# Attention scores contracted over 66 and 96 partitions in place of a zero-padded 128

## The reference

```python
# first stack, layer 0: forgetting attention, 8 heads of 64
s = einsum("bqhd,bkhd->bhqk", q, k) * 64**-0.5
s = s + cum[:, :, lo:hi, None] - cum[:, :, None, :hi]   # decay, a term of the query and one of the key
p = softmax(where(causal, s, -1e30));  o = p @ v
...
# second stack, layers 0 and 1: 8 query heads of 96, 2 key groups, three branches
s_cmp = q_c . kc ;  o_cmp = softmax(s_cmp) @ vc          # 31 compressed keys
s_slc = q_c . k_slc ; s_win = q_c . k_win                # causal; with 512 tokens both cover all keys
o = g0 * o_cmp + g1 * o_slc + g2 * o_win
```

## Time and profile before

| | |
|---|---|
| time, median of 3 runs | 3630.98 us (3629.97 to 3632.04) |
| the profiled execution's own time | 3629.97 us |
| its span in the profile | 3628.2 us |
| TensorE busy | 3544.8 us, 98% of the span |
| VectorE, ScalarE, GpSimd busy | 1464.8, 1194.2 and 54.3 us |
| mean granted TensorE clock | 0.979 of full speed |

### The profile page before, as it was taken

One profiled execution on the slowest core, in us unless ns is written; L12 is line 12 of the kernel. 1 busy time (PEld: TensorE's weight loads), 2 busy tenths in 40 slices (PEclk: granted clock), 3 DMA queues, 4 the chain that ended last, 5 costly groups with the idle time before them and its releaser, 6 DMA issues.

```text
span 3628.2 us, 39774 instructions
## 1 busy us (share of the span) xinstructions
PE 3544.8 (98%) x17601; PEld 2981.9 (82%) x17601; DVE 1464.8 (40%) x1604; ACT 1194.2 (33%) x1755; POOL 54.3 (1%) x66
## 2 busy tenths in 40 slices
PE   8999999999999999999999899999999999899999
PEld 7778788888888888888888778888888888788887
DVE  4444433337644323322344454223422354553233
ACT  3344332236534222322233343222322332432222
POOL 2000000000000000000000000000000000000000
PEclk9999999999999999999998799999999998899999
DMA  5214132223341322232223102322332222013321
GB/s 158 93 47 146 52 116 93 105 76 99 105 140 61 108 93 97 87 119 93 94 80 104 47 12 93 105 93 93 105 102 96 93 78 83 24 36 121 99 93 58
DMA packets 246333, 326.44 MB, mean 90 GB/s; under 512 B 18320, under 2 KB 215232, under 8 KB 246160
## 3 DMA queue, kind: packets, MB, share of 16 engines
q1 hardware_dynamic: 241232, 308.77, 26.3%
q0 software_dynamic: 4928, 15.12, 1.2%
HBM read 321.74 MB, written 2.10 MB: 89 GB/s over the span
## 4 chain that ended last, share of the span: by engine, by line
PE 91%; DVE 5%; ACT 4%; DMA 0%; issue 0%; POOL 0%; DVEq 0%; ACTq 0%; POOLq 0%
PE P L483 27%; PE P L484 27%; PE P L485 27%; PE P L488 3%; PE P L631 3%; PE P L609 3%; DVE WR L1429 1%; ACT WR L954 1%; DVE BIG L1437 1%; ACT BIG L961 1%; DVE BIG L1446 1%; DVE HT L1437 1%; ACT XN L961 0%; PE P L868 0%; ACT BC L961 0%
## 5 line engine op out<-in xcount | busy, mean ns | idle before, releaser
L1429 DVE TENSOR_TENSOR WR<-STG,WR 128x2048 fp32r<-128x2048 f32 (+2 forms) x300 | 669.5, 2232 | 1382.1 <-ACT WR L954 1381.8
L483 PE MATMUL P<-HT,WR 128*128 128x512 f32 (+1 forms) x3016 | 1126.4, 373 | 5.5 <-DVE WR L1429 3.0
L484 PE MATMUL P<-HT,WR 128*128 128x512 f32 (+1 forms) x3016 | 1122.9, 372 | 0.0
L485 PE MATMUL P<-HT,WR 128*128 128x512 f32 (+1 forms) x3016 | 1122.6, 372 | 0.0
L954 ACT CAST WR<-STG 128x2048 fp32r<-128x2048 f32 (+2 forms) x300 | 557.5, 1859 | 1102.1 <-PE P L485 1101.9
L483 PEld LDWEIGHTS P<-HT,WR 128*128 128x128 f32 x3016 | 571.3, 189 | 105.2 <-DVE WR L1429 3.8
L485 PEld LDWEIGHTS P<-HT,WR 128*128 128x128 f32 x3016 | 570.9, 189 | 98.4
L484 PEld LDWEIGHTS P<-HT,WR 128*128 128x128 f32 x3016 | 571.2, 189 | 97.4
L483 PE MATMUL P<-WR,HT 128*128 128x512 f32 (+1 forms) x1344 | 524.6, 390 | 12.3 <-DVE HT L1437 12.3
L485 PE MATMUL P<-WR,HT 128*128 128x512 f32 (+1 forms) x1344 | 521.6, 388 | 0.0
L484 PE MATMUL P<-WR,HT 128*128 128x512 f32 (+1 forms) x1344 | 521.3, 388 | 0.0
(11 more groups left out here) (177 smaller groups left out, 2522.8 us busy)
## 6 DMA issues: line engine op xcount, KB each, us to landing
STG<-in_w_ffn_gu_dram SPq DMA_DIRECT2D x44, 1024.0 KB, 5.0
STG<-in_ffn_w_gate_dram SPq DMA_DIRECT2D x44, 1024.0 KB, 5.3
STG<-in_ffn_w_up_dram SPq DMA_DIRECT2D x44, 1024.0 KB, 5.3
STG<-in_ffn_w_down_dram SPq DMA_DIRECT2D x44, 1024.0 KB, 4.9
STG<-in_w_ffn_down_dram SPq DMA_DIRECT2D x22, 1024.0 KB, 4.8
STG<-in_w_xkv_dram SPq DMA_DIRECT2D x16, 1024.0 KB, 5.4
STG<-in_w_in_dram SPq DMA_DIRECT2D x12, 1024.0 KB, 5.2
STG<-in_w_xq_dram SPq DMA_DIRECT2D x8, 1024.0 KB, 5.2
```

The source lines that it names most:

```text
L483: pe.matmul(o, lh, rh, start=first, stop=False)
L484: pe.matmul(o, lh, rl, start=False, stop=False)
L485: return pe.matmul(o, ll, rh, start=False, stop=last)
L1429: v.tensor_tensor(WR[0:p, n % NWR, 1, cut], STG[0:p, n % NSTG, cut], WR[0:p, n % NWR, 0, cut].bitcast(F32), ALU.subtract).then_inc(ve.sem, ...
```

## The change

The score products of fox read rows 0 to 65 of queries and keys alone, and those of n0 and n1 rows 0 to 95 alone. The memsets of the zeros go, and so do the two waits of GpSimd that kept the ones behind the zeros in fox, GpSimd's wait ahead of the zeros in n0 and n1, and TensorE's wait for these zeros. The products' columns, their number and their order stay.

```diff
-        N_QP = BIG[:, 0:4096].rearrange("p (h n) -> p h n", h=8)
-        N_KP = BIG[:, 4096:6144].rearrange("p (z g n) -> p z g n", z=2, g=2)
...
-                         qk=[(F_QA[:, h, tcol(t)], F_KA[:, h, 0:128 * (t + 1)])],
+                         qk=[(F_QA[0:66, h, tcol(t)], F_KA[0:66, h, 0:128 * (t + 1)])],
...
-                         qk=[(N_QP[:, h, tcol(t)], N_KP[:, br, h // 4, 0:128 * (t + 1)])],
+                         qk=[(N_Q[:, h, tcol(t)], N_K[:, br, h // 4, 0:128 * (t + 1)])],
...
             g.wait_ge(*ve.at("positions"))
-            po.memset(F_QA[64:128, :, :], 0.0).then_inc(pw_zero.sem, pw_zero.up("zeros_q"))
-            g.wait_ge(*pw_zero.at("zeros_q"))
             po.memset(F_QA[64:66, :, :], 1.0).then_inc(pw_zero.sem, pw_zero.up("ones_q"))
             g.wait_ge(*ve.at("fox", "yb", 3))
-            po.memset(F_KA[64:128, :, :], 0.0).then_inc(pw_zero.sem, pw_zero.up("zeros_k"))
-            g.wait_ge(*pw_zero.at("zeros_k"))
             po.memset(F_KA[64:66, :, :], 1.0).then_inc(pw_zero.sem, pw_zero.up("ones_k"))
...
-                    if part == 1:
-                        g.wait_ge(*ve.at(before, "slot", 21))
-                        po.memset(BIG[96:128, 0:6144], 0.0).then_inc(pw_zero.sem, pw_zero.up("zeros", s))
...
                 scores(0)
-                g.wait_ge(*pw_zero.at("zeros", s))
                 last_turn = attend(s, lambda it: ve.at(s, "k", 2), ve.at(s, "v", 3), hook)
```

## The result

| | median of the runs | lowest to highest |
|---|---|---|
| before | 3631.21 us (9) | 3626.55 to 3632.07 |
| after | 3665.44 us (9) | 3640.06 to 3667.96 |

The ratio is 1.0078, 95% interval 1.0055 to 1.0100: slower by 0.8%. The nine executions of the changed program are not spread evenly: six lie between 3664 and 3668 us, three between 3640 and 3650. The profiled one took 3667.70 us, 37.7 more than the profiled one of before.

What follows compares the result with a forecast made beforehand. TensorE, busy 98% of the span, was taken as the bound, its clock deciding. From the profiled 3629.97 us, fox +36 and n0 and n1 +20 gave 3686, so 3687 us as median; range 3640 to 3775, forecast case 3660 to 3705.

Steps and rivals of the forecast that it cites:

- The clock is what the change moves: TensorE in the three attentions: matmuls on fewer rows hold the clock up less; working theory behind fox +36, layers +20.
- Fox +36: Fox's attention: clock does not come back at 181.1, only in the output projection; 34.2 us plus 2 there.
- as long as before: Sign of being right: everything outside the three attentions keeps its length and is only shifted.
- n0 and n1 +20: Attentions of n0 and n1 at 96 rows: lost islands 12 us, later final rises 6, new falls 2.
- the islands: Full-clock stretches between half-clock ones in n0 and n1; lost whole they cost 23.6 us, taken as 12.
- later rises and falls: n0 and n1: final clock rise comes later, 6 us together; clock falls again later, 2 us together.
- The third of my three losses: n0 and n1: clock may fall again later at a group of L885; 1 us per layer, 2 together.
- The memsets and waits at 0: Removed memsets and waits in fox, n0 and n1: priced at 0, between a gain of 3.5 us and nothing.
- no effect: Rival: clock goes by busy time or counts 66 or 96 rows as full; time stays 3631 us; 12%.
- faster: Rival: score products in all three attentions cost in proportion to rows, saving 28 us: 3603 us; 3%.
- the weight-load rule: TensorE: a weight load goes by its columns, not rows of contraction; by this alone the change moves nothing there.

Runs made afterwards that it cites:

- the rows alone: Kernel before with only the score products' operands cut to 66 rows in fox and 96 in n0 and n1, all memsets and waits kept: 3666.45 us, ratio 1.0089.
- fox alone: Kernel before with only fox's score products cut to 66 rows, n0 and n1 at 128, memsets and waits kept: 3640.29 us, ratio 1.0051.
- n0 and n1 alone: Kernel before with only the score products of n0 and n1 cut to 96 rows, fox at 128: 3636.87 us, ratio 1.0014.
- the change with the kick: Changed kernel plus four extra constant products, 128 rows by 512 columns, after steps 7 to 10 of fox's attention: 3638.89 us, ratio 1.0022.
- more columns: Kernel before with compressor products of n0 and n1 reading 124 columns in place of 62: 3604.21 us, ratio 0.9931; again 3603.34 us, ratio 0.9926.

## Why the prediction was right, and what of it was not

*The clock is what the change moves:* shown. Around fox TensorE is at half clock for 99.0 us in place of 13.7, and the loss is there with every memset and wait kept (the rows alone: ratio 1.0089 against 1.0078). That it is the rows, zeros or not, that hold the clock is shown for fox by 96 rows against 66 and 80. Why the clock goes by them is open.

*Fox +36:* the sum was 34.2 to the end of the attention and 2 in the projection. In the profile of the change it is 37.6 to the end of the attention and 2.4 from there to x0, 40.0 together, with the clock back at 266.4 where I said about 260. I rested this on the reading that 60% of TensorE's time before the rise is in the very products that lose rows. What I had not seen is that the return varies from one execution to the next: it is at 241.6 in the profile of the rows alone and at 210.6 in the one with 80 rows, and ten of 28 executions with 66 rows take only 3632 to 3650. The clock that stays down to the projection is seen in two profiles, of the change and of fox alone, both of the larger group; but the profile that came back at 241.6 is of that group too, and no execution with 66 rows of the smaller group was profiled.

*Luck.* Of the nine runs of the change six fell into the larger group; with fox alone it was four of nine, and the median 3640.29. Had the change fallen so, its median would have lain below my own range of 3660 to 3705. And the other stages were not "as long as before": those between fox and n0 gave 4.2 us back, which hides that fox cost more than I said.

*n0 and n1 +20:* this is the term that was mis-sized. Measured: 0.1 us in the profile of the change, 5.3 with n0 and n1 alone (ratio 1.0014), 9.7 in the profile of the rows alone. The direction was right, the price was not. I charged 0.9 of TensorE's work in the islands, took half of that, and added 8 us for later rises and falls. With n0 and n1 alone, 10.2 us more at half clock in n0 before the last rise cost, with a short fall after it, 5.2 us; but a lost island of the same length turned up once with 128 rows as well and cost 3.5 us there, so the 96 rows need not be what took it. And in the profile of the change the islands only moved: in n0 the sum at half clock was even 3.5 us smaller, and in n1 6.8 us more of it cost nothing. The third of my three losses, a fall behind a group of L885 in the later items, is the one that only profiles with 96 rows show. With that term at its measured 0 to 10, the forecast would have been 3667 to 3677; the larger group is at 3664 to 3671.

*The memsets and waits at 0:* shown by the kernel that keeps them. GpSimd's idle time before it sends the negated sum is 8.64 us after the change where it was 5.06: the 3.5 us went into a wait.

```profile
92.53 3.52 POOL L420 MEMSET BIG<- 2x4096 f32 x1 [43.64 <-DVE XN L1427]
104.69 0.52 POOL L423 DMA_DIRECT2D BIG<-BIG  x1 [8.64 <-DVE CUM L1439]
```

*The rival "no effect"* rested on the clock following busy time, as the Trainium skill has it (TensorE: Matmul & The Clock Gate, The HAM clock gate). The compressor's windows, 100% busy ahead of the fall and 100% busy at 0.54 across it, speak against that reading. The rival "faster" falls: 512 columns take 608 ns with 96 rows as with 128. What I called agreement of the trace with the weight-load rule rested on times of matmuls. The rule of the Trainium skill (TensorE: Matmul & The Clock Gate, LDWEIGHTS), that a weight load does not go by the rows of contraction, agrees with the times of the loads themselves: at full clock 192 ns with 128 rows (before), 191 with 96 (the change), 191 with 66 (the change with the kick), and 186 with 31.

## What to carry to other kernels

Before you trim zero rows or idle columns off a matmul, look at the granted clock around it: here they cost TensorE no time, and they were what kept it at full clock. The place to look is where TensorE is busy, small products follow a sparse stretch, and the clock is just coming back. Where a stage is fully busy and still at half clock, try giving the products more rows or columns, up to where they would get longer; here more columns were worth 28 us, some 20 of them in the stage itself. And take several runs and more than one profile before you read a few us off a stage whose clock goes up and down.

## What the runs showed that I had not expected

One program can have two times: at 66 or 80 rows in fox, 25 of 38 executions are above 3664 us and 13 between 3629 and 3650, though TensorE runs the same instructions. With 96 rows all ten lie within 5.1 us. And rows of zeros count: with 30 more rows of zeros every execution took the time of the kernel before, and in the profiled one the clock in fox was back at 191.1.
